# Transposes of the probabilities placed ahead of the next scores in each attention unit

## What is computed

```python
def mixer_dilated(h, w_qkv, q_gain, k_gain, w_o, cos, sin):      # layer A
    ...
    scores = jnp.einsum('rnqhd,rnkhd->rnhqk', qr, kc) * ATTN_SCALE  # per window
    ...
    p = jnp.exp(scores - m[..., None])
    den = p.sum(axis=-1)
    num = jnp.einsum('rnhqk,rnkhd->rnqhd', p, vc)
    ...
    return attn.reshape(B, S, N_HEADS * HEAD_DIM) @ w_o

def second_block(x, ...):
    for i in range(DEPTH_2):
        hn = rmsnorm_2(x, attn_norm[i])
        x = x + (mixer_dilated if i % 2 == 0 else mixer_moba)(hn, ...)
        hn = rmsnorm_2(x, ffn_norm[i])
        x = x + conv_ffn(hn, ...)
```

## Time and profile before

| | |
|---|---|
| median of 3 runs | 1156.03 us (1153.71 to 1156.86) |
| profiled execution: its own time | 1157.73 us |
| profiled execution: span of its trace | 1155.9 us |
| mean granted clock of TensorE in it | 0.979 of full |
| PE busy | 1115.3 us, 96% of the span |
| DVE busy | 788.3 us, 68% |
| ACT busy | 646.7 us, 56% |
| share of PE in the chain that ended last | 87% |

### The profile page before, as it was taken

The page is one execution under the profiler, slowest core; times in us unless marked ns, Lnnn a source line. Parts: engine busy times, 40 slices in busy tenths (PEclk is TensorE's granted clock), DMA queues, the critical chain, the costliest instruction groups (busy, mean ns, idle before and its releaser), DMA issues.

```text
span 1155.9 us, 19015 instructions
## 1 busy us (share of the span) xinstructions
PE 1115.3 (96%) x6928; PEld 969.3 (84%) x6928; DVE 788.3 (68%) x1435; ACT 646.7 (56%) x1122; POOL 12.9 (1%) x22
## 2 busy tenths in 40 slices
PE   7998789999998999999999999999999999999998
PEld 5876679998987887888878999999876769999997
DVE  5767566555557667576674687787874746887776
ACT  5364455454456555655575665555666556655554
POOL 0000100000000000000000000000000000000000
PEclk9997689999999999999999999999999999999999
DMA  9552045655644655046541456556552515565562
GB/s 324 149 182 73 26 132 183 189 182 186 193 147 148 213 180 165 25 147 203 161 146 46 156 184 208 190 168 195 169 177 74 185 56 179 182 199 182 165 203 106
DMA packets 117037, 184.33 MB, mean 159 GB/s; under 512 B 6640, under 2 KB 70384, under 8 KB 116720
## 3 DMA queue, kind: packets, MB, share of 16 engines
q1 hardware_dynamic: 116688, 183.23, 50.0%
q10 hardware_dynamic: 288, 0.29, 0.1%
HBM read 182.45 MB, written 1.05 MB: 159 GB/s over the span
## 4 chain that ended last, share of the span: by engine, by line
PE 87%; DVE 6%; ACT 5%; issue 2%; DMA 1%; SPq 0%; DVEq 0%; ACTq 0%
PE ps L679 10%; PE ps L681 10%; PE ps L680 10%; PE ps L655 10%; PE ps L657 9%; PE ps L656 9%; PE ps L738 5%; PE ps L739 5%; PE ps L740 5%; PE ps L832 2%; PE ps L815 2%; PE ps L797 2%; ACT w_hi L1117 1%; PE ps L858 1%; PE ps L755 1%
## 5 line engine op out<-in xcount | busy, mean ns | idle before, releaser
L1624 DVE TENSOR_TENSOR w_lo<-w_stage,w_hi 128x1024 fp32r<-128x1024 f32 x336 | 403.1, 1222 | 191.3 <-ACT w_hi L1117 190.4
L1117 ACT ACTIVATE w_hi<-w_stage 128x1024 fp32r<-128x1024 f32 x336 | 347.7, 1053 | 182.7 <-PE ps L657 86.6
L679 PE MATMUL ps<-aT_hi,w_hi 128*128 128x256 f32 x992 | 282.2, 284 | 0.7 <-DVE aT_lo L1638 0.7
L680 PE MATMUL ps<-aT_lo,w_hi 128*128 128x256 f32 x992 | 281.2, 283 | 0.0
L681 PE MATMUL ps<-aT_hi,w_lo 128*128 128x256 f32 x992 | 281.2, 283 | 0.0
L655 PE MATMUL ps<-w_hi,aT_hi 128*128 128x512 f32 x480 | 194.2, 405 | 3.9 <-DVE w_lo L1697 2.2
L679 PEld LDWEIGHTS ps<-aT_hi,w_hi 128*128 128x128 f32 x992 | 190.8, 192 | 2.3 <-issue 1.0
L680 PEld LDWEIGHTS ps<-aT_lo,w_hi 128*128 128x128 f32 x992 | 190.9, 192 | 1.0
L681 PEld LDWEIGHTS ps<-aT_hi,w_lo 128*128 128x128 f32 x992 | 190.8, 192 | 0.0
L657 PE MATMUL ps<-w_hi,aT_lo 128*128 128x512 f32 x480 | 190.1, 396 | 0.0
L656 PE MATMUL ps<-w_lo,aT_hi 128*128 128x512 f32 x480 | 190.0, 396 | 0.0
(11 more groups left out here) (220 smaller groups left out, 1165.9 us busy)
## 6 DMA issues: line engine op xcount, KB each, us to landing
w_stage<-in_ffn_w_up SPq DMA_DIRECT2D x88, 512.0 KB, 4.7
w_stage<-in_a_w_qkv SPq DMA_DIRECT2D x72, 512.0 KB, 4.1
w_stage<-in_ffn_w_down SPq DMA_DIRECT2D x44, 512.0 KB, 3.5
w_stage<-in_w_up SPq DMA_DIRECT2D x32, 512.0 KB, 3.8
w_stage<-in_w_down SPq DMA_DIRECT2D x32, 512.0 KB, 4.2
w_stage<-in_w_in SPq DMA_DIRECT2D x24, 512.0 KB, 4.7
w_stage<-in_b_w_qkv SPq DMA_DIRECT2D x24, 512.0 KB, 4.5
w_stage<-in_w_out SPq DMA_DIRECT2D x8, 512.0 KB, 3.8
```

The source lines that it names most:

```text
L679: pe.matmul(o, wh, aT_hi[:, k, :], start=(k == 0), stop=False)
L680: pe.matmul(o, wh, aT_lo[:, k, :], start=False, stop=False)
L1117: act.activation(w_hi[:, slot, :], w_in[:, slot, :], ACT.Copy).then_inc(hi_done[slot], 1)
L1624: dve.tensor_tensor(w_lo[:, slot, :], w_in[:, slot, :], w_hi[:, slot, :].bitcast(F32), ALU.subtract).then_inc(lo_done[slot], 1)
```

## The change

In PE's loop the block that issues S(u+1) moves from ahead of T(u-1) to behind it. A step was S(u+1), T(u-1), V(u-2) and is now T(u-1), S(u+1), V(u-2). No instruction is added or removed, and no other engine's program changes. Since the block moves two lines up, the transposes are at L813 in the changed kernel, where L815 was before.

```diff
                 n = len(units)
                 for u in range(1, n + 2):
-                    if u + 1 < n:
-                        scores(stg, units[u + 1], u + 1)
                     if u <= n:
                         v = u - 1
                         for h in range(2):
                             b = bank(stg, f"p{'AB'[h]}{v}")
                             pe.wait_ge(*is_free(stg, f"p{'AB'[h]}{v}"))
                             pe.wait_ge(s["prob"], at(stg, "prob", 2 * v + h + 1))
                             for t in range(len(units[v]["values"])):
                                 last = pe.transpose(ps[:, b, t * P:(t + 1) * P],
                                                     score_ring[v % 3][:, h, t * P:(t + 1) * P], ident)
                             last.then_inc(full[b], 1)
+                    if u + 1 < n:
+                        scores(stg, units[u + 1], u + 1)
                     if u >= 2:
                         v = u - 2
```

## The result

The changed kernel takes 1179.51 us (median of 4 runs, 1177.72 to 1181.73) against 1156.44 us for the kernel before in the same comparison (1153.71 to 1158.08): a ratio of 1.0201, 95% interval 1.0179 to 1.0222, 23 us slower. The forecast was 1174, with a range from 1167 to 1184. The profiled execution has a span of 1177.6 us, 21.7 more than before.

A forecast was written before the change was run, and what follows sets the result against it. PE, busy 96% of the span, was taken to bound the kernel. Layer A's 10.7, layer B's 2.93 twice and the clock's 1.4 made 18.0 us over the median of 1156.03: 1174 us, range 1167 to 1184.

The forecast's parts named there:

- The mechanism and its chain: Attention loops: T_B waits for DVE's copyB, queued behind maxima that need the later S(u+1); 3.29 us from S in layer A.
- The stall: Layer A, steady step: PE idles 0.55 us in front of T_B, waiting for DVE's copy of bank 5.
- a loop of layer A: Each of layer A's two loops takes 5.34 us more, 10.7 together; a step becomes 3.88 in place of 3.34.
- a loop of layer B: Each of layer B's two loops takes 2.93 us more; two steps take 4.16 in place of 3.40.
- The 0.06 us from copy to transposes: Time from the end of DVE's copy to the T_B that waits for it, read in half_b0.
- PE's waits for copyB: Sign in the trace: T waits for copyB, 0.4 to 0.7 us each, six times per layer A loop, about three in B.
- S(2)'s cover: Loop start: S(2) no longer runs in the wait ahead of T(0); 1.08 of the 5.34 us in layer A.
- The clock: Loop starts: more idleness lowers PE's clock; one new fall beside the one kept, +1.4 us, bounded by -1.43 and +4.3.
- the rival that I gave 14%: Attention loops: three or more clock falls beyond the count, each up to 1.43 us, giving 1179 to 1186 us; 14%.
- The stall isn't hidden: Rival, layer A: copy reaches bank 5 within PE's own 2.74 us, so time stays within 0.3%; 3%.
- nothing was faster: Rival: early copies close every PE gap in the loops, 5.2 us, giving 1150.8 us; 1%.
- The clock did not stay low throughout: Rival, attention loops: clock low throughout, PE steps up to twice as long, 41 us more, about 1215 us; 3%.

The follow-up runs named there:

- e5: The changed kernel with the matmuls of S(2) issued once more, as spare work, ahead of T(0): 1173.59 us.
- e7: The kernel before with the change made in layer B's two loops alone: 1163.37 us, ratio 1.0073 to before.
- e4: The changed kernel with S(2) alone put back ahead of T(0); transposes come first from step 2 on: 1170.91 us.
- e12: The changed kernel with ACT's 1.06 us split of one quarter of weights, and DVE's part, moved into step 8 of the loop: 1163.69 us.

## Why the prediction was right, and where its size was off

**The mechanism and its chain** were as predicted. The stall was put at 0.55 (0.54 measured), a step of layer A at 3.88 (3.87), a loop of layer A at 5.34 more (5.28 in half_a1 at full clock), and a loop of layer B at 2.93 (2.83: 15.19 less 12.36, seen at full clock in e5 and e7). The 0.06 us from copy to transposes, which I took from one row of half_b0, held (0.05). PE's waits for copyB are 16, where six in each loop of layer A and three in each of layer B make 18: in the loops at the lower clock PE's own work takes longer and fills some of the stalls. The four loops at full clock come to 16.2 us against 16.6 in the sum.

**S(2)'s cover** is in those numbers. e4, which gives it back, saves 1.56 in a loop of layer A (27.92 less 26.36), against 1.6 for the cover (1.08) and one stall (0.55). The agreement is in part luck, since e4 has a wait for ACT of 1.23 in place of that stall.

**The clock** is the term that was mis-sized. I counted one fall kept and one new, +1.4 us. By the loops it was 3.17 in half_a0 (31.09 less 27.92), 3.32 in half_b0 (18.51 less 15.19) and 2.27 in half_b1 (17.46 less 15.19) less the 1.41 it already had, 7.4 in all: 6 us more than in the sum, against which the chains came out 0.3 less. That is, to 0.1, the 5.5 us by which the median lies above the forecast. Two things were off. There were three falls where I counted two. And each cost more than the 1.43 read from the kernel before: in the changed half_a0 the clock was at the lower level for all of the 10 us from 462.5 to 472.5, where it was for 3 us in half_b1 before. In that stretch S takes 1.9 to 2.1 us in place of 1.1, and since S stands in the chain to the copy, the fall is paid there in part even while PE has idle time. The prediction put every fall at the 1.43 of one that lasted 3 us; nothing in it said how long the next would last.

The time lies just above my forecast of 1169 to 1179 and inside the range, at the lower edge of the rival that I gave 14%. That rival's own reason did not come true: it asked for three or more falls beyond my count at up to 1.43 each, and there was one more, and longer ones. With one fall a loop it could not have come true as I wrote it, since two of the four loops were counted already. That the range held with the clock off by 6 us is in part luck.

**The rivals.** The stall isn't hidden, and nothing was faster. The clock did not stay low throughout: by the rule of the Trainium skill (TensorE: Matmul & The Clock Gate, Part 4) that transposes don't count as busy, that case was nearer; half_a1 of the changed kernel ran at 1.00 with 10.2 of PE's 24.9 busy us in transposes, and so did all four loops of e12 (10.3 of 25.0 in layer A), so here it did not decide.

**Which idleness matters** I had half right: I named the idle starts, and then feared the steady stalls for the range. In the runs every fall came behind an idle start of 1.3 us or more, and stalls alone brought none in the six loops of layer A in e4, e5 and e12. Once the clock was low, though, it stayed low for longer in the loops with stalls, so the fear was not for nothing. What decides whether an idle start of 1.3 or 1.7 us is followed by a fall (21 of 30) stays open: half_a0 and half_a1 have the same program, and I made no run that shifts one against the other.

## What to carry to other kernels

Before reordering one engine, write down the fixed orders of the engines that serve it. A copy that frees a buffer may stand, in its own engine's queue, behind work that needs the instruction being delayed, and the price can be added up from a steady step: producer to first reader, its length, the copy, the release. Here that sum was right to 0.1 us in a loop.

An idle stretch of PE that seems to cost only itself should be priced with the clock that follows it. Moving 1.06 us of unrelated work, and its own wait for PE, out of the way of the first transposes gained 6.7 us in four places.

## What the hardware showed unexpectedly

Filling idle time of PE with matmuls whose result is thrown away made the kernel 5.9 us faster (1173.6 against 1179.5); 3.2 of it is the loop of half_a0, which it kept at full clock.

Stalls of 0.54 us in each step of 3.87 lowered the clock in none of the loops of e4, e5 and e12 in layer A, while 1.7 us at once, ahead of T(0), were followed by stretches at 1.2 GHz, up to 10 us long, in 5 of 8 loops of layer A and 7 of 8 of layer B, and 1.3 us in 9 of 14.
